# Two expert stages: whole-array work in one block a unit, down product two units late, down weights in halves, first weights loaded during routing

## What is computed

```python
def _expert_choice_moe(h, w_router, w1, w3, w2):
    cap = EC_CAPACITY * T // N_EXPERTS            # 128 tokens for each of 16 experts
    aff = jax.nn.softmax((h @ w_router).astype(F32), -1)
    gate, idx = lax.top_k(jnp.swapaxes(aff, 1, 2), cap)
    xe = h[bidx, idx]
    he = jax.nn.silu(jnp.einsum('becd,edf->becf', xe, w1)) * jnp.einsum('becd,edf->becf', xe, w3)
    ye = jnp.einsum('becf,efd->becd', he, w2) * gate[..., None].astype(h.dtype)
    return jnp.zeros_like(h).at[bidx, idx].add(ye)
```

## Time and profile before

| | us |
|---|---|
| median of 3 runs | 4055.1 (4053.34 to 4060.05) |
| the profiled execution | 4048.3 |
| its span, first to last instruction | 4046.4 |

### The profile page before, as it was taken

How to read it: one execution, slowest core, us unless ns; L and a number is a source line. 1 busy time by engine, 2 the same in 40 slices (tenths; PEclk the granted TensorE clock), 3 DMA queues, 4 the chain that set the end, 5 groups by cost and what they waited for, 6 DMA issues and landing times. The chain is left out here.

```text
span 4046.4 us, 63749 instructions
## 1 busy us (share of the span) xinstructions
PE 3658.5 (90%) x26142; PEld 2221.3 (55%) x26142; DVE 2560.2 (63%) x3457; ACT 883.0 (22%) x1752; POOL 460.1 (11%) x500
## 2 busy tenths in 40 slices
PE   6999899987869999999999998999976998858995
PEld 3444488873345555555555554644455898425552
DVE  5656389984855766666666663555166778457773
ACT  2000022210111221221212211312126443012232
POOL 0000000003100000000000000200031875001110
PEclk9999999998989999999999999999988999979997
DMA  7564133216479899898998895412002100229995
GB/s 284 217 253 163 62 132 119 104 42 246 198 276 349 304 316 325 306 319 304 313 323 305 311 313 196 149 48 81 31 1 83 40 4 4 106 95 318 341 337 197
DMA packets 288986, 800.71 MB, mean 198 GB/s; under 512 B 17481, under 2 KB 24657, under 8 KB 273873
## 3 DMA queue, kind: packets, MB, share of 16 engines
q1 hardware_dynamic: 270720, 720.06, 49.5%
q0 software_dynamic: 17280, 74.59, 5.8%
q10 hardware_dynamic: 720, 2.17, 0.2%
HBM read 709.60 MB, written 87.16 MB: 197 GB/s over the span
## 5 line engine op out<-in xcount | busy, mean ns | idle before, releaser
L1518 PE MATMUL banks<-moe_down,moe_hidT 128*128 128x512 f32 x1280 | 580.0, 607 | 42.6 <-DMA moe_down<-d_wd 41.2
L1518 PEld LDWEIGHTS banks<-moe_down,moe_hidT 128*128 128x128 f32 x1280 | 240.8, 193 | 347.1 <-issue 334.6
L1880 PE MATMUL banks<-hT,w_in_ring 128*128 128x512 f32 (+3 forms) x976 | 363.9, 535 | 2.4 <-ACT hT L1941 1.3
L1499 PE MATMUL banks<-moe_wsums,moe_xsums 128*64 128x256 f32 x2560 | 306.4, 387 | 42.2 <-DVE moe_xsums L1630 27.0
L512 PE MATMUL banks<-hT,w_in_ring 128*128 128x512 f32 x768 | 339.3, 597 | 1.6 <-PEq L212 1.6
L1880 PEld LDWEIGHTS banks<-hT,w_in_ring 128*128 128x128 f32 (+1 forms) x976 | 183.3, 189 | 181.1 <-issue 170.0
L1499 PEld LDWEIGHTS banks<-moe_wsums,moe_xsums 128*64 128x64 f32 x2560 | 177.2, 138 | 185.6 <-issue 111.0
L1587 ACT COPY moe_parts<-banks 128x512 f32<-128x512 f32 (+1 forms) x240 | 123.4, 514 | 659.3 <-PE banks L1499 657.9
L512 PEld LDWEIGHTS banks<-hT,w_in_ring 128*128 128x128 f32 x768 | 143.1, 190 | 185.2 <-issue 175.7
L1642 DVE TENSOR_TENSOR moe_wsums<-x_block 128x2048 f32<-128x2048 f32 x40 | 91.7, 2292 | 155.9 <-PE banks L1499 155.9
L1674 DVE TENSOR_TENSOR moe_hid<-moe_silu,moe_parts 64x512 f32<-64x512 f32 x160 | 110.0, 687 | 108.0 <-ACT moe_silu L1607 105.4
(11 more groups left out here) (479 smaller groups left out, 6053.6 us busy)
## 6 DMA issues: line engine op xcount, KB each, us to landing
moe_down<-d_wd SPq DMA_DIRECT2D x80, 2048.0 KB, 11.1
moe_raw<-d_wg SPq DMA_DIRECT2D x80, 1024.0 KB, 7.0
moe_raw<-d_wu SPq DMA_DIRECT2D x80, 1024.0 KB, 10.3
x_block<-d_wg SPq DMA_DIRECT2D x80, 1024.0 KB, 9.0
x_block<-d_wu SPq DMA_DIRECT2D x80, 1024.0 KB, 11.5
w_in_ring<-d_w_in SPq DMA_DIRECT2D x9, 2048.0 KB, 10.1
x_normed<-d_mod_w SPq DMA_DIRECT2D x8, 2048.0 KB, 12.6
d_taps<-dft SPq DMA_DIRECT2D x8, 2048.0 KB, 7.4
```

The costliest lines, as they stand in the source:

```text
L1499: last = nc.tensor.matmul(m.ps[out, bank, at], tokens(k), weights(kind * HK + k), start=(k == 0), stop=(k == HK - 1))
L1518: last = nc.tensor.matmul(m.ps[:, Y_BANK + h, :], hidT[:, i * P:(i + 1) * P], wd[:, i, h * BANK:(h + 1) * BANK], start=(fc == 0 and i == 0 ...
L1880: last = nc.tensor.matmul(m.ps[0:width, g % 6, 0:n], ring[:, q % 2, k, at:at + width], hT[:, k, first:first + n], start=(k == 0), stop=(k ...
```

## The change

- In `experts_stage` TensorE does all seven products of unit n in a row, and after them, in one block, what uses the whole array: the second half of the next expert's rows (if the unit ends an expert), the transposes of the hidden values of unit n - 1, `back` of unit n - 2 (it was n - 1), and the first half of the rows of the expert after the next (they were the next one's). `hidT` gets a second buffer.
- The down weights come in two transfers of 1 MB, each with a semaphore for its arrival and one for its release. `back` waits for each half and tells when it is done with it (`d_half`, `d_mm`). The loads of unit n - 3 follow the gate and up loads of unit n.
- The gate and up weights of unit 0 are loaded by `mixer_out_stage`, after the router product, into `hT`; `experts_stage` uses that memory as its first `raw` buffer in place of one of its own. Unit 1's are issued when the first gather has landed.
- ScalarE and VectorE follow this order; `combine` goes before `token_sums`; GpSimd gathers a fourth expert ahead. Each odd expert's result (`leaving`) now waits until the scatter of the expert just before has landed (it was the one before that).
- Both stages, moe1 and moe2, are changed, as they are one function. The numbers of products, transposes, sums and bytes stay.

```diff
@@ mixer_out_stage, SyncE
             if deep:
                 for n in range(5, LATE_SLOTS):
                     late(n)
+            sp.wait_ge(s.logit_mm, 1)
+            for a in range(2):
+                load_gate_up(sp, expert_weights(hT), d_gate[0], d_up[0], a, slice(0, EW), m.first_raw[a])
             sp.wait_ge(s.stored, TT * 16)
@@ experts_stage, SyncE
-            def load_down(fc, e):
-                sp.dma_start(wd[:], pick(d_down, e)[:, fc * (EW // P):(fc + 1) * (EW // P), :]).then_inc(s.wd, 16)
+            def load_down(fc, e, n):
+                for h, free in ((0, s.d_half), (1, s.d_mm)):
+                    if after_first(n):
+                        sp.wait_ge(free, n)
+                    at = fc * (EW // P) + h * HALF_DOWN
+                    sp.dma_start(wd[:, h * HALF_DOWN:(h + 1) * HALF_DOWN, :], pick(d_down, e)[:, at:at + HALF_DOWN, :]
+                                 ).then_inc(wd_in[h], 16)
...
+                    if whole and n == 1:
                         sp.wait_ge(gathered[0], 16)
+                    for a, done in ((0, 5), (1, 7)):
+                        if not whole or n >= 2:
+                            sp.wait_ge(s.p_mm, turn * (PRODUCTS * FU) + PRODUCTS * (j - 2) + done)
+                        if not whole or n >= 1:
+                            load_gate_up(sp, raw[j % 2], pick(d_gate, e), pick(d_up, e), a, cols, raw_in[j % 2][a])
+                    if whole and n == 1:
+                        load_down(0, 0, 0)
+                    elif not whole or n >= 4:
+                        load_down((j - 3) % nf, at[(j - 3) // nf], n - 3)
@@ experts_stage, TensorE
-            def back(fc, n, e):
+            def back(j, n, e):
+                fc = j % nf
                 pe.wait_ge(s.ht, n + 1)
-                pe.wait_ge(s.wd, n * 16 + 16)
                 if fc == 0 and after_first(e):
                     pe.wait_ge(s.y_read, e)
-                for i in range(EW // P):
-                    for h in range(2):
-                        last = nc.tensor.matmul(m.ps[:, Y_BANK + h, :], hidT[:, i * P:(i + 1) * P],
...
-                last.then_inc(s.d_mm, 1)
+                for half, done in ((0, s.d_half), (1, s.d_mm)):
+                    pe.wait_ge(wd_in[half], n * 16 + 16)
+                    for i in range(half * HALF_DOWN, (half + 1) * HALF_DOWN):
+                        for h in range(2):
+                            last = nc.tensor.matmul(m.ps[:, Y_BANK + h, :], hidT[:, j % 2, i * P:(i + 1) * P],
...
+                    last.then_inc(done, 1)
@@ body
                     product(P65_BANK, RIGHT, xsum(1), t(0))
-                    if following:
-                        rows(*following, 0)
...
                     product(P34_BANK, RIGHT, x(1, HIGH), t(2))
                     if started or j:
-                        turned(n - 1)
                         pe.wait_ge(s.copied, copied)
                     product(PAIR_BANK, RIGHT, x(0, LOW), w(0, LEFT))
-                    if following:
-                        rows(*following, 1)
                     product(P7_BANK, LEFT, xsum(3), w(0, RIGHT))
                     product(PAIR_BANK, LEFT, x(1, LOW), w(1, LEFT))
                     product(P34_BANK, LEFT, xsum(4), w(1, RIGHT))
+                    if following:
+                        rows(*following, 1)
                     if started or j:
-                        back((j - 1) % nf, n - 1, turn * EU + (j - 1) // nf)
+                        turned(n - 1)
+                    if started or j > 1:
+                        back(j - 2, n - 2, turn * EU + (j - 2) // nf)
+                    if beyond:
+                        rows(*beyond, 0)
                 if final:
                     turned(N - 1)
-                    back(nf - 1, N - 1, E - 1)
+                    for n in (N - 2, N - 1):
+                        back(n, n, n // nf)
@@ VectorE
                     if not (final and j == FU - 1):
                         weight_sums(turn + (j + 1) // FU, (j + 1) % FU)
+                    combine(turn, j)
                     following = next_expert(turn, j, final)
                     if following:
                         token_sums(*following)
-                    combine(turn, j)
                     activate(n)
...
+                    last = j - 2
+                    if last % nf == nf - 1 and (started or last >= 0):
+                        leaving(turn, last // nf)
```

More of the change, by code:

```diff
@@ L1442, in _ @@
                 load(turn)
-            for n in (N - 2, N - 1):
-                sp.wait_ge(s.d_mm, n)
-                load_down(n % nf, n // nf)
+            for n in range(N - 3, N):
+                load_down(n % nf, n // nf, n)
         @block.gpsimd
@@ L1701, in body @@
                 if final:
-                    leave(1, E - 1, N, (TURNS - 1) * (EU * 16))
+                    for eu in range(EU):
+                        if (eu + 1) * nf + 1 >= FU:
+                            leaving(turn, eu)
             gate_v(v, diag)
```

117 lines of the change are left out of this document (58 added, 59 removed).

## The result

The changed kernel takes **3958.8 us** in the median of four runs (3954.9 to 3962.4), the kernel before 4057.3 us in four runs on the same chip (4053.3 to 4060.1). The ratio is **0.9767, interval 0.9751 to 0.9784**: 2.3% faster. The forecast was 3961 us with a range of 3940 to 4004. The profiled execution took 3955.2 us, its span is 3953.3 us; against the 4046.4 us of the one before that is 93.1 us less, where the sum was 93.6. (The medians are 98.5 us apart; what follows explains the two profiled executions.)

The account below looks back on a forecast made before the run. Moe1 was taken as bound by TensorE, moe2 by TensorE with DMA close behind. Terms summed to 93.6, say 94 us, off the profiled 4048.3: 3954; for the median, 6.8 us above, 3961 us, range 3940 to 4004.

Parts of the forecast that it names:

- first weights, moe1 and moe2: Stage starts: loading unit 0's weights during routing brings the first product 15.6 us sooner in moe1, 12.7 in moe2.
- switches in moe1: Putting whole-array work next to back saves 0.31 us per transpose group: 63 hidden and 30 row groups, 28.8 us.
- small waits for down weights: Nine small TensorE waits in moe1 go with halves loaded for a down product two units late: 5.8 us.
- the long stall: Moe1's 8.60 us wait behind 5.2 MB queued for the next stage stays but shrinks: 4.5 us, between 0 and 10.5.
- ramp of moe1: First units of moe1: back(0)'s idle and slow matmuls go, VectorE holds others up: 4 us, between 0 and 8.
- end of moe1: Last down products of moe1: one back more, but only 1 MB halves in flight: 6.6 us gained.
- units of moe2: Units take 20.8 us instead of 21.52, the queue nearly full: 9 us over 13 units, between 0 and 12.
- ramp of moe2 (2 and -2.4): First units of moe2: two shorter units gain 2 us; late row sums cost 2.4, between -6 and 3.
- end of moe2 with what follows: Last down products of moe2 and the last row store, which waits for the scatter before: 7.0 us gained.
- rival 3: In the block, transposes and back pay a switch among themselves: 78 us gained, 3977 us; chance 0.05.
- rival 2: The starts don't come, routing held up as long or the gather as slow: 66 us gained, 3989 us; chance 0.10.
- Rival 4: Down weights in 1 MB pieces make the DMA engines worse: kernel slower, 4150 us at 5 us more a unit; chance 0.05.

Follow-up runs that it names:

- experiment 2: Changed kernel with the hidden transposes moved back between the third and fourth product: 3987.3 us, ratio 0.9847 to the kernel before.
- Experiment 4: Changed kernel with the block kept but the down product one unit late instead of two: 4052.7 us, ratio 1.0005 to the kernel before.
- experiment 6: Changed kernel with the 5.2 MB fetched in moe1 for the next stage issued in three pieces: 3950.5 us, ratio 0.9747 to the kernel before.
- experiment 1: Changed kernel with unit 0's gate and up weights loaded at the experts stage's start, not during routing: 3984.0 us, ratio 0.9837 to the kernel before.
- Experiment 5: Changed kernel with half the matmuls of each gate and up product left out, all transfers kept: 3746.7 us, ratio 0.9254 to the kernel before.
- Experiments 10: Changed kernel with token rows transposed, copied and summed earlier in moe2's first two units, ScalarE's copies ahead of the silu: 3950.2 us, ratio 0.9757.
- 11: Changed kernel with next-stage loads spread, spare room for moe1's last two down weights, moe1's TensorE loop written out, early moe2 rows: 3916.5 us, ratio 0.9674.
- experiment 3: Changed kernel with each unit's down weights in one 2 MB transfer, still two units late: 4013.1 us, ratio 0.9903 to the kernel before.

## Why the prediction was right, and where it wasn't

All in us gained; the measured ones are worked out from the marks, the starts of the down products and, where named, an experiment. A down product that left the ramp and went to the end counts 7.06 in both. Two of the 63 groups of hidden transposes lie in the ramp of moe1 and are counted there.

| term | forecast | measured |
|---|---|---|
| first weights, moe1 and moe2 | 15.6 + 12.7 | 15.85 + 13.05 |
| switches in moe1 | 28.8 | 30.6 |
| small waits for down weights | 5.8 | 8.0 |
| the long stall | 4.5 | 4.2 |
| ramp of moe1 | 4 | 2.7 |
| end of moe1 | 6.6 | 6.75 |
| units of moe2 | 9 | 12.2 |
| ramp of moe2 (2 and -2.4) | -0.4 | -5.2 |
| end of moe2 with what follows | 7.0 | 8.2 |
| way back of the loop | - | -1.2 |
| stages that aren't touched | 0 | -2.1 |
| sum | 93.6 | 93.1 |

- **The block.** The switch was taken from the earlier trace rows as 0.31; a group of hidden transposes saves 0.35 (experiment 2 brings back 20.04 to the hundredth), a group of row transposes 0.30 (it cost 0.74 and costs 0.44). The bound that transposes and `back` might pay among themselves (rival 3) is out by the 0.44 us between them. But the prediction called the copy of the hidden values hidden "beside other work" in half a sentence. Experiment 4 shows that this cover carries everything: without it the kernel is the old one.
- **Small waits.** They all went. The sum held only the idle time (14.4 - 8.6); the intervals of before were 6.4 us too long in those nine places, and 1.6 us more in four others where the profile names no down weights.
- **The long stall** stayed, smaller, as said; experiment 6 shows its cause and removes it.
- **The starts.** Each is within 0.4 us, and rival 2 is out by experiment 1. A serial chain in which each link has a row can be added up link by link.
- **Units of moe2.** I took 20.8 between TensorE's 20.6 and what I feared of the queue; it is TensorE's own, 20.57 us. This is the step that was too careful: a DMA share of 1.00 was read as nearly the end. Experiment 5 shows 1.04 at 374 GB/s held for 200 us. The forecast share of 1.03 for moe2 was wrong in the same way: it stayed at 1.00, with 351 GB/s instead of 340.
- **The ramp of moe2** is the term that was mis-sized, by 4.8 us. The idle time was seen for one unit (3.3 us, and it is 4.6) and not for the next (2.3 more). That two products behind a gap run slower, 3.9 us in all, was in no term, though the earlier trace rows show the same behind their waits (9.94 and 9.36 instead of 7.13). Experiments 10 and 11 show what another order brings back: 3.5 and 6.1 us.
- **The ends** came out as forecast: 1 MB lands in 5.1 us at the end of moe1, the estimate to the tenth, and in 4.8 to 4.9 in moe2. The 2 us that the estimate took as the fixed part of a landing stood in no row of before; 8.0 us for 2 MB and 5.1 for 1 MB now make it 2.2. The Trainium skill, "DMA: Bandwidth & Descriptors", section Bandwidth, gives 6.15 us of engine time for 1 MB issued from GpSimd; an estimate by it was 4 us of gain in moe1 instead of 6.6. The measured 6.75 decides against it for these transfers, which SyncE issues. What the prediction missed is how much hangs on the halves: experiment 3 makes the two ends 39 us longer.
- **Rival 4**, the slower case (1 MB pieces make the DMA engines worse), is out: the share rose only with the rate, and 2 MB pieces lose 55 us.

The low and high terms nearly cancel (the units and switches of both stages 5.0 above, the ramp of moe2 4.8 below), so the sum is better than its parts; no part was off by more than 5 us. That forecast and measurement agree to 0.5 us is luck: the ramp of moe1 and the untouched stages alone differ by more between runs of the same instructions. Two readings in the prediction were slightly off, without effect on the sum beyond 0.3 us: the stretch of moe2 in the earlier trace rows is eight units and not nine, and the last down product of moe1 ended 25.1 us after the 2480.6 named there, not 25.3.

Open remain the untouched stages, which differ by 3 us between the two kernels and by up to 8 us among all the runs (moe1's end to the ranking of block 2), and the ramp of moe1 up to its first down product, which is between 43.8 and 50.8 us in runs with the same instructions there. The 2.7 us of the ramp of moe1 in the table are therefore one draw of several; that of moe2, first product to first down product, is 53.2 to 53.7 us in the four runs that have the same instructions and loads there.

## What to carry to other kernels

Gathering operations of one array shape saves a small, countable price per switch (here 0.35 us for 63 groups and 0.30 us for 30 in moe1), but only together with a lag that keeps their results off the path: look first for who reads the result, and how soon. A deeper lag moves work to the end of the stage, where nothing covers a load: cut these loads in pieces, or give the last ones room of their own. And take the floor of an engine from a run that is bound by it, not from a busy share of 1.00.

## What the hardware showed that I had not expected

- **The way back of a long loop.** In a hardware loop of TensorE over eight units (about 1070 matmuls and transposes) each way back costs 3.2 to 4.0 us, in two gaps, the second a few us into the new turn; straight code for all 64 units has none. The median falls by 24.7 us with it, of which the five ways back are 18.6. The loop of two units in moe2 (about 280) shows no gap. The Trainium skill, "Advanced Engine Details and Errata", section Control Flow Timing, gives about 51 ns for a branch; by it, as an estimate, the five would cost 0.3 us in all, and the trace shows 18.6. That the instructions of the loop's head have to be fetched anew would fit both, but no run here shows it.
- **Short gaps cost twice.** Gaps of 1.1 to 2.9 us in the ramp of moe2 are followed by products at a granted clock of 0.60 to 0.68, which adds 1.6 to 2.3 us to each pair of products; behind waits of 1.1 to 2.1 us at the ends the last down product takes 7.10 us in most runs and 8.80 in some.
- **A DMA share of 1.03 at 383 GB/s** holds for 800 us on this one core, from loads of 1 MB with indirect stores among them.
